# Differential attention in a streaming encoder step: the samples' four heads as one stacked unit, moved between the second and third block

## What is computed

```python
def diff_sample(q, k, v, k_cache, v_cache, lam):
    k_all = jnp.concatenate([k_cache, k], axis=1)      # 128 cached keys + 32 new
    v_all = jnp.concatenate([v_cache, v], axis=1)
    sc = jnp.einsum('bqhcd,bkhcd->bhcqk', q, k_all).astype(jnp.float32) * scale
    p = jax.nn.softmax(sc, axis=-1)                    # 4 heads, 2 components c each
    a = p[:, :, 0] - lam * p[:, :, 1]
    return jnp.einsum('bhqk,bkhv->bqhv', a, v_all)
...
od = rms_norm(od, diff_norm_w) * (1.0 - lambda_init)   # per head, over 128 values
y = jnp.concatenate([yc, yd], axis=-1) @ w_out         # yc: gated half, yd: differential half
```

## Time and profile before

| | |
|---|---|
| runs | 1221.92, 1221.89, 1221.46 us; median 1221.89 us |
| the profiled execution: its time, its span | 1221.92 us, 1219.7 us |
| PE busy | 1202.8 us, 99% of the span |
| DVE, ACT, POOL busy | 730.4, 307.0, 800.6 us |
| the stage, from the first score to the first matmul of L613 | 699.05 to 791.11 us of the span |

### The profile page before, as it was taken

One profiled execution on the slowest core, in us unless ns is written; L12 is line 12 of the kernel. 1 busy time (PEld: TensorE's weight loads), 2 busy tenths in 40 slices (PEclk: granted clock), 3 DMA queues, 4 the chain that ended last, 5 costly groups with the idle time before them and its releaser, 6 DMA issues.

```text
span 1219.7 us, 23497 instructions
## 1 busy us (share of the span) xinstructions
PE 1202.8 (99%) x8618; PEld 1141.1 (94%) x8618; DVE 730.4 (60%) x1267; ACT 307.0 (25%) x639; POOL 800.6 (66%) x953
## 2 busy tenths in 40 slices
PE   8999999999999999999999998999999999999997
PEld 8997999999999999999999986999999999999997
DVE  6766678776777622127444679687777777741112
ACT  4035332222222200003112167443222222210001
POOL 7962676767676677778655423577777766677772
PEclk9999999999999999999999999999999999999999
DMA  6321223232222232324231311232222222232321
GB/s 222 96 87 36 72 87 92 87 98 86 86 86 86 87 103 87 103 87 125 85 98 56 107 35 35 89 104 97 86 86 86 86 86 86 92 94 92 104 87 74
DMA packets 36072, 109.07 MB, mean 89 GB/s; under 512 B 6160, under 2 KB 8848, under 8 KB 36016
## 3 DMA queue, kind: packets, MB, share of 16 engines
q1 hardware_dynamic: 29232, 102.14, 26.8%
q10 hardware_dynamic: 6784, 6.12, 1.7%
HBM read 103.12 MB, written 5.13 MB: 89 GB/s over the span
## 4 chain that ended last, share of the span: by engine, by line
PE 94%; DVE 2%; ACT 2%; issue 1%; POOL 1%; DMA 0%; SPq 0%; POOLq 0%; DVEq 0%; ACTq 0%
PE psum L643 18%; PE psum L641 12%; PE psum L642 12%; PE psum L644 12%; PE psum L645 9%; PE psum L613 6%; PE psum L615 6%; PE psum L614 6%; PE psum L1164 1%; PE psum L1166 1%; PE psum L1165 1%; PE psum L951 1%; PE psum L892 1%; PE psum L1133 1%; PE psum L931 1%
## 5 line engine op out<-in xcount | busy, mean ns | idle before, releaser
L513 POOL TENSOR_TENSOR w_lo<-w_raw,w_hi 128x512 fp32r<-128x512 f32 x354 | 488.1, 1400 | 14.8
L643 PE MATMUL psum<-h_both,w_hi 128*128 128x480 f32 x704 | 267.0, 379 | 0.0
L466 POOL TENSOR_TENSOR tick<-tick 1x1 f32<-1x1 f32 x183 | 44.1, 241 | 317.7 <-PE psum L645 204.4
L508 POOL TENSOR_SCALAR w_hi<-w_raw 128x512 fp32r<-128x512 f32 x354 | 219.1, 632 | 0.0
L641 PE MATMUL psum<-h_both,w_hi 128*128 128x304 f32 x704 | 215.4, 306 | 0.0
L642 PE MATMUL psum<-h_both,w_hi 128*128 128x304 f32 x704 | 212.8, 302 | 0.0
L644 PE MATMUL psum<-h_both,w_lo 128*128 128x304 f32 x704 | 210.9, 300 | 0.0
L645 PE MATMUL psum<-h_both,w_lo 128*128 128x240 f32 x704 | 191.5, 272 | 0.0
L645 PEld LDWEIGHTS psum<-h_both,w_lo 128*128 128x128 f32 x704 | 131.8, 187 | 20.5
L613 PE MATMUL psum<-h_both,w_hi 128*128 128x272 f32 x488 | 143.4, 294 | 0.1
L615 PE MATMUL psum<-h_both,w_lo 128*128 128x272 f32 x488 | 141.2, 289 | 0.0
(11 more groups left out here) (325 smaller groups left out, 2460.3 us busy)
## 6 DMA issues: line engine op xcount, KB each, us to landing
w_raw<-in_weights SPq DMA_DIRECT2D x184, 512.0 KB, 3.5
x<-in_x SPq DMA_DIRECT2D x8, 272.0 KB, 6.1
w_raw<-in_weights SPq DMA_DIRECT2D x3, 384.0 KB, 5.8
out_diff_v_new<-odd_dv ACTq DMA_DIRECT2D x1, 1024.0 KB, 6.2
out_diff_k_new<-odd_kT ACTq DMA_DIRECT2D x1, 1024.0 KB, 5.0
out_y<-y_one SPq DMA_DIRECT2D x2, 456.0 KB, 2.5
even_rope<-in_rope ACTq DMA_DIRECT2D x1, 544.0 KB, 4.6
odd_rope<-in_rope ACTq DMA_DIRECT2D x1, 544.0 KB, 4.1
```

The lines of the kernel that those rows point to most:

```text
L466: pool.tensor_tensor(tick[:, :], tick[:, :], tick[:, :], ALU.mult).then_inc(ticks, 1)
L508: ins = pool.tensor_scalar(w_hi[:, k, part], w_raw[:, k % RAW, part], 1.0, 0.0, ALU.mult, ALU.add)
L513: ins = pool.tensor_tensor(w_lo[:, k, part], w_raw[:, k % RAW, part], w_hi[:, k, part].bitcast(F32), ALU.subtract)
L643: pe.matmul(two, wh, both[:, :, ONE:T], start=first, stop=False)
```

## The change

The samples' four heads become one unit. Its scores are stacked in PSUM: head h takes the rows 32h to 32h + 31, so the unit is a full 128 rows by 160 keys, and maxima, exponentials, normalisation, transposes and copy are done once for all heads. The values remain apart for each head, now with 128 rows of keys in both parts: rows 32 to 127 of the new values (`o_dv[:, 4]`) are set to zero beforehand by DVE (`padded`), and ACT waits for that before it copies values there. The order of blocks becomes 0, 1, samples, 2, 3 (`ODD_ORDER`), so there are 17 units and steps, the samples are unit 8, and block 3 is the last. The samples have norm buffers of their own, `ODD_FILL` is dealt anew over 17 steps, and 16 tiles instead of 11 are left behind the last unit, eight on either side of the last head sums. The first chunk of the second half of the output projection is written out in two halves: columns 0 to 271 wait for blocks 0 to 2 and the samples, columns 272 to 543 for block 3.

```diff
-        OU = [(b, h) for b in range(5) for h in range(4)]
-        ODD_BATCHES = [(0, 1), (2, 3), (4, 5), (6, 7), *((u,) for u in range(8, 16)), (16, 17), (18, 19)]
+        ODD_ORDER = (0, 1, 4, 2, 3)
+        OU = [(b, h) for b in ODD_ORDER for h in range(4 if b < 4 else 1)]
+        ODD_BATCHES = [(0, 1), (2, 3), (4, 5), (6, 7), *((u,) for u in range(8, 17))]
...
-        ODD_FILL = [(0, 6, 4), (1, 1, 4), (0, 3, 2), (1, 1, 3), (1, 2, 2), (4, 0, 1), (1, 3, 0), (2, 6, 1),
...
+        ODD_FILL = [(0, 9, 3), (1, 1, 0), (1, 1, 2), (2, 0, 1), (7, 2, 0), (0, 6, 0), (3, 1, 0), (3, 0, 5),
...
...
+        BLOCK_AT = {b: i for i, b in enumerate(ODD_ORDER)}
+        LAST_UNIT = {b: u for u, (b, _) in enumerate(OU)}
+        COPY_AT = {LAST_UNIT[b] + 1: b for b in ODD_ORDER}
+        SUMS_AT = {LAST_UNIT[b] + (2 if b < 4 else 3): b for b in ODD_ORDER}
+        RSTD_AT = {u + 1: b for u, b in SUMS_AT.items()}
+        HIGH_AT = {u + 2: b for u, b in SUMS_AT.items()}
...
+        def head_buffers(b):
+
+            return (head_t, sq_h, r_h) if b < 4 else (head_s, sq_s, r_s)
...
                 for c in (1, 0):
                     rows = slice(64 * c, 64 * c + 64)
+                    if b == 4:
+                        for head in range(4):
+                            ins = pe.matmul(psum[SMP * head:SMP * (head + 1), bank + c, at_:at_ + nk],
+                                            d_qT[rows, head, SEQ:T], d_kT[rows, head, k0:k0 + nk], start=True, stop=True)
+                        ins.then_inc(s_ready, 1)
+                        continue
...
+                if b == 4:
+                    for head in range(4):
+                        at_ = head * SMP
+                        for kb in range(2):
+                            v = d_vc[:, head * P:(head + 1) * P] if kb == 0 else o_dv[:, 4, head * P:(head + 1) * P]
+                            ins = pe.matmul(psum[:, 4, at_:at_ + SMP], v,
+                                            d_probsT[u % 2][:, kb * P + head * SMP:kb * P + (head + 1) * SMP],
+                                            start=kb == 0, stop=kb == 1)
+                    ins.then_inc(o_ready, 1)
+                    return
...
-            odd_values(19)
+            odd_values(len(OU) - 1)
             odd_fill(odd_rest[0], len(HALF_TILES) - 8)
-            odd_head_sums(4)
+            odd_head_sums(3)
             odd_fill(len(HALF_TILES) - 8, odd_rest[1])
-            pe.wait_ge(y_lo_done, 9 + 5)
-            for m in range(KC):
-                if m:
-                    pe.wait_ge(x_upd, X_ODD + KC + m - 1)
...
+            for half in range(2):
+
+                pe.wait_ge(y_lo_done, 9 + (5 if half else 4))
...
+                    o(ve.memset(o_dv[:, 4], 0.0), padded)
```

More of the change, by code:

```diff
@@ L359, in build @@
         odd_at, odd_end, gate_step, count = {}, {}, {}, 0
-        for u in range(-1, 20):
+        for u in range(-1, len(OU)):
             for place in range(3):
@@ L1137, in odd_head_sums @@
             def odd_head_sums(b):
-                nq = TILES[b][1]
-                pe.wait_ge(hsq_ready, 5 + b + 1)
-                pe.matmul(psum[:, 5, 0:4 * nq], ones, sq_h[:, 0:4 * nq], start=True, stop=True).then_inc(head_sum, 1)
+                w = 4 * TILES[b][1]
+                pe.wait_ge(hsq_ready, 5 + BLOCK_AT[b] + 1)
+                pe.wait_ge(hrms_ready, 5 + BLOCK_AT[b])
+                pe.matmul(psum[:, 5, 0:w], ones, head_buffers(b)[1][:, 0:w], start=True, stop=True).then_inc(head_sum, 1)
             def half_tile(item, k):
@@ L1192, in _ @@
                     odd_batch(ODD_NEXT[u])
-                if h == 1 and b >= 1:
-                    odd_head_sums(b - 1)
+                if u in SUMS_AT:
+                    odd_head_sums(SUMS_AT[u])
                 odd_fill(*odd_at[u, 2])
-            odd_values(19)
+            odd_values(len(OU) - 1)
             odd_fill(odd_rest[0], len(HALF_TILES) - 8)
-            odd_head_sums(4)
+            odd_head_sums(3)
             odd_fill(len(HALF_TILES) - 8, odd_rest[1])
-            pe.wait_ge(y_lo_done, 9 + 5)
-            for m in range(KC):
-                if m:
-                    pe.wait_ge(x_upd, X_ODD + KC + m - 1)
+            s = S_ODD_OUT + 4
+            pe.wait_ge(w_ready, s + 1)
+            for half in range(2):
+                pe.wait_ge(y_lo_done, 9 + (5 if half else 4))
+                cols = slice(half * HALF, (half + 1) * HALF)
+                for c in range(4):
+                    wh, wl = w_hi[:, s % RING, c * P:(c + 1) * P], w_lo[:, s % RING, c * P:(c + 1) * P]
+                    pe.matmul(psum[:, half, 0:HALF], wh, d_hi[:, c, cols], start=c == 0, stop=False)
+                    pe.matmul(psum[:, half, 0:HALF], wh, d_lo[:, c, cols], start=False, stop=False)
+                    ins = pe.matmul(psum[:, half, 0:HALF], wl, d_hi[:, c, cols], start=False, stop=c == 3)
+            ins.then_inc(mid_done, 1)
+            for m in range(1, KC):
+                pe.wait_ge(x_upd, X_ODD + KC + m - 1)
                 out_chunk(S_ODD_OUT + 4 + m // 2, m, 2 + m % 2, d_hi, d_lo, 0)
@@ new lines, in odd_turned, with head_copy, head_squares @@
+                ac.activation(d_probsT[u % 2][:, 0:n], psum[:, ODD_TURN[u], 0:n], ACT.Copy).then_inc(pT_out, 1)
+            def head_copy(b):
+                w = 4 * TILES[b][1]
+                ac.wait_ge(o_ready, 10 + LAST_UNIT[b] + 1)
+                if 0 < b < 4:
+                    ac.wait_ge(y_lo_done, 9 + BLOCK_AT[b - 1] + 1)
+                ac.activation(head_buffers(b)[0][:, 0:w], psum[:, 4, 0:w], ACT.Copy).then_inc(head_out, 1)
+            def head_squares(b):
+                w = 4 * TILES[b][1]
+                ac.wait_ge(head_out, BLOCK_AT[b] + 1)
+                if b < 4:
+                    ac.wait_ge(head_sum, 5 + BLOCK_AT[b])
+                ac.activation(head_buffers(b)[1][:, 0:w], head_buffers(b)[0][:, 0:w], ACT.Square).then_inc(hsq_ready, 1)
@@ L1592, in _ @@
                     gate_silu(gate_step[u - 1])
-                if h == 0 and b >= 1:
-                    head_copy(b - 1)
-                    head_squares(b - 1)
-                if h == 2 and b >= 1:
-                    head_rstd(b - 1)
-                if h == 3 and b >= 1:
-                    head_hi(b - 1)
+                if u in RSTD_AT:
+                    head_rstd(RSTD_AT[u])
+                if u in HIGH_AT:
+                    head_hi(HIGH_AT[u])
+                if u in COPY_AT:
+                    head_copy(COPY_AT[u])
+                    head_squares(COPY_AT[u])
                 if u - 2 in gate_step:
                     gate_hi(gate_step[u - 2])
-            head_copy(4)
-            head_squares(4)
-            head_rstd(4)
-            head_hi(4)
+            head_copy(3)
+            head_squares(3)
+            head_rstd(3)
+            head_hi(3)
             dma(io["state_new"][:, 0], o_st[:, 0], out_done)
@@ L2210, in _ @@
                     odd_max(u + 2)
-                if h == 2 and b >= 1:
-                    head_scale(b - 1)
-                if h == 3 and b >= 1:
-                    head_low(b - 1)
+                if u in HIGH_AT:
+                    head_low(HIGH_AT[u])
+                if u in RSTD_AT:
+                    head_scale(RSTD_AT[u])
                 if u - 2 in gate_step:
```

82 lines of the change are left out of this document (34 added, 48 removed).

## The result

The changed kernel takes 1215.19 us (median of 5 runs, 1214.83 to 1215.32) against 1221.67 us (5 runs, 1221.46 to 1221.92): 6.5 us less, ratio 0.9945 with an interval from 0.9935 to 0.9956. The forecast was 1217.0. Its profiled execution took 1215.32 us with a span of 1213.1 us, 6.6 less than the span of before.

A forecast was written before the change was run, and what follows sets the result against it. PE, busy for 1202.8 of 1219.7 us, was taken as the bound. Less PE work (2.1 us) and less idle time (2.8) made 4.9 us off 1221.92: 1217.0, own range 1215.6 to 1219.0, wide range 1215.0 to 1219.8.

The forecast's parts named there:

- PE's work therefore falls by 2.1 us (ends -0.1 and 2.6): Stage from first score to end of fill: cheaper samples' scores, values and transposes take 2.1 us off PE's busy time.
- I take 1.2: Samples' stacked scores: 16 passes with entry cost 1.2 us against 1.7 before, saving 0.5 (ends -1.0 and 0.8).
- I take 2.0: Samples' values: 16 passes of 128 rows cost 2.0 us; with 0.26 for transposes, 1.6 saved of 3.9.
- The idle time falls from 5.1 to 2.3 us: PE's idle time in the stage falls by 2.8 us, ends 0.5 and 4.0.
- The wait at the values of unit 9: Step 10: PE reaches these values at 5.2, ACT's samples' copy is done at 5.7, a new wait of 0.5 us.
- The 0.9 at the transposes of unit 11: Unit 11 is ready at 9.1 us, PE gets there at 8.2: 0.9 us of wait.
- The tail: Behind the last head sums: block 3's norm takes 4.6 us, PE has 4.5 us of work; counted as 0.
- Without that half, the wait would be 1.6: Tail: without the first half of the next chunk as PE work, PE would wait 1.6 us.
- PE's work hardly falls: Rival: strips don't overlap and values stay at 0.17 a pass; saving 2.7 us, 1219.2, chance 0.10.
- the waits only move: Rival: copy behind the silu and steps 9 to 12 keep 4.5 us idle; 1220.1 us, chance 0.14.
- The one that ended slower: Rival: a late silu in step 9 holds up ACT's queue and both copies; about 1225 us, chance 0.03.
- overlap of all strips and short waits: Best case: 2.6 us of PE work and 4.0 of waits saved, 6.6 together; 1215.3 us, chance 0.10.

The follow-up runs named there:

- the doubling: Changed kernel with every samples' score matmul issued a second time into the same place, 32 passes instead of 16: 1215.12 us (one run).

## Why the prediction was off where it was

The sign and the mechanism were right: the time came from less work of PE and from less idle time, all in this stage. The time lies at the fast end of the wide range and 0.4 us outside the forecast's own (1215.6 to 1219.0), 1.8 us below the value, and one term of the sum carries the miss.

**"PE's work therefore falls by 2.1 us (ends -0.1 and 2.6)" is the step that failed:** PE's busy time in the stage fell by 3.8, beyond the upper end.
- *Scores: "I take 1.2", saved 0.5.* Measured from the last fill matmul (721.51, less its own 0.13) to the head sums (722.16): 0.52 us, so 1.2 were saved. The step "I take 1.2, nearer to rows 7" overrated the cost: rows 7 have two strips of columns, and with four the passes cost 0.02 us each, as the doubling showed. Even the low end, 0.9, which assumed four at a time, was too dear. The Trainium skill ("TensorEngine Tiling (Array Packing)", Key Properties) lets different tiles load and multiply in parallel; the trace agrees, and more closely than the sum believed.
- *Values: "I take 2.0", saved 1.6 with the transposes.* The 16 passes took 1.80, and the two transposes with their entry about 0.3, so 1.8 were saved. The reason given, that the array isn't switched to 32 rows, is shown twice (0.8 us each time). The Trainium skill ("TensorE: Matmul & The Clock Gate", LDWEIGHTS) gives 0.107 us for loading the weights of a pass, 128 columns, whatever the rows; the passes start at 0.11 apart (737.09 to 738.89, 16 of them), so here the rule was the better guide than the row of 128 columns at 0.127.
- These two make 3.0 of the 3.8. Two costs that the sum put at nothing make most of the rest. The first is the fill's start: a unit was measured up to the first fill matmul behind it, 777.62, but the next one follows that only 0.23 us later instead of 0.126 (first row below). Four units make 0.4; as not every unit costs the 0.97 us of the one measured, together some 0.3.
- The second is the matmul ahead of a wait. It isn't overlapped by the next one, and its full time counts as busy: 747.13 to 747.69 are 0.56 us, the row counts 0.27 of them as idle, so the last fill matmul takes 0.29 and not 0.126. Over all eight waits of the kernel before this comes to about 1.0 us, over the three of the kernel after to 0.6, by the same reading of their timelines: 0.4. No run tests the two costs.

```profile
777.85 0.29 PE L1165 MATMUL psum<-y_both,w_hi 128*128 128x272 f32 x1
```

```profile
747.13 0.29 PE L1166 MATMUL psum<-y_both,w_lo 128*128 128x272 f32 x1
747.69 0.55 PE L1184 MATMUL psum<-consts,diff_probs 128*128 128x128 f32 x3 [0.27 <-DVE diff_probs L2157]
```

**"The idle time falls from 5.1 to 2.3 us" held:** 5.1 to 2.2, all of it before block 3. That it came out to a tenth is partly luck, since its parts were off in both directions. The list of waits that it started from also lacks the two for turned probabilities, 0.7 us (above). The wait at the values of unit 9 was named with its cause; it is 1.0 instead of 0.5, not because of ACT, which had copied the samples' results at 742.46, 5.7 us after the step began at 736.76, as forecast, but because PE, with its shorter values, was there at 4.7 instead of 5.2. The 0.9 at the transposes of unit 11 did not come, nor did most of the 0.4 before 718.50 (0.1): ACT copies unit 10 at 742.71, 6.0 after the step's start as forecast, but from there to unit 11's transposes (745.23) the chain takes 2.5 us and not the 3.1 that the sum gave it. The 0.2 at the transposes of unit 8 were not foreseen. The gate's low part, "should be in time", was not: 0.7, behind the DVE instruction of 1.80 us. The three runs that moved a copy, the gate's parts and two tiles suggest why the sum was safer than its parts: ACT is busy without a break through these steps, and their total stays within 0.3 us, whichever instruction of PE waits. On DVE the long instruction moved in the same way, from the gate's part to the norm's multiply, when the two changed places.

**The tail** was counted at 0 and is 0: the last fill matmul starts at 784.44 and the new chunk at 784.56, its second half at 786.07. "Without that half, the wait would be 1.6": unsplit the stage was 0.9 us longer, with 0.7 as the wait shown, since the norm was through sooner: DVE's two instructions took 0.75 and 0.69 us there, not the 1.00 and 1.21 of the earlier trace rows. What the prediction did not see is how much the tail hangs on the order of the queues: with the stacked unit last, in the one order that was run, nearly all of the gain is given back.

**The rivals.** That PE's work hardly falls is refuted by the busy time, that the waits only move by the idle time. The one that ended slower looked at the right place, ACT's queue in step 9, but the wait there is 1.0 us and not several. The case nearest to the result is "overlap of all strips and short waits" (6.6 us, 1215.3, chance 0.10): its total came true, but not its parts: more work saved (3.8 for 2.6) and fewer waits (2.9 for 4.0) than it said.

## What to carry to other kernels

The scores of small heads that are stacked so that their matmuls use different strips of rows and of columns cost little on PE (0.02 us a pass here); where a tile must be shallow, ask whether padding it to the depth of its neighbours is cheaper than the change of shape, and whether the place is covered by a wait anyway. Try the short unit where the chain over ACT and DVE falls behind PE; if it goes to the end, look first at which engine's queue its norm stands in. When a wait of PE comes from an engine that is busy without a break, expect reordering to move it rather than to remove it, as the runs that moved the copy and the two tiles showed here. And a change that leaves waits of nearly 2 us between matmuls can lose more by the clock than by the waits: in the run that was moved and not stacked 4.0 us of busy time against 2.0 of idle time.

## What the runs showed of the hardware that I had not expected

- Passes of 64 x 32 (160 columns moving, fp32) in two strips of rows and four of columns: 0.02 us for each additional one, 0.07 in two strips of rows alone (0.30 us for 16, 0.57 for 8).
- Passes of 128 rows with 32 moving columns start 0.11 us apart (16 in 1.80 us); between 128 and 32 rows each change adds 0.1 us (2.58 us for 16).
- The same DVE subtraction of 128 x 544 takes 0.72 us, but 1.78 to 1.82 where POOL had begun a subtraction for `w_lo` 0.4 to 0.6 us before it (1.80 at 746.96 in the kernel after, 1.82 at 731.05 and 1.78 at 749.54 in the kernel before; POOL from 746.47, 730.63 and 749.05). The cause wasn't tested.
- In the run that was moved and not stacked, the granted clock was at 0.50 for 6 us after a wait of only 1.7 us had followed a busy stretch, and 272-column matmuls went from 0.126 to 0.226 us apart. With the unit last it was at 0.91 from 786.23 to 800.00, behind a wait of 2.4 us. The waits of up to 1.5 us in the profiled execution of the run with the unit between the third and fourth block left it at 0.999 over the span; the four other runs of that kernel, whose waits aren't known, show 0.997.
